# A two-block transformer kernel: the first gate and up pair reads x times scale, TensorE sums the shift's modulation weights, VectorE adds the squares

## The chip, the cores and the metric

The kernel runs on one core of one Trainium2 chip, in one launch. The metric is the device time of that launch in microseconds (us): 1558.38 us is the median of three timed runs of the kernel before (1555.36 to 1558.40). The profiled execution, from which all rows below come, took 1553.17 us, of which 1551.5 us are the span between its first and last recorded instruction.

## The reference, cut to what matters

The whole function is a first block (modulated SwiGLU, a hybrid mixer, a second SwiGLU) and a second block, for 512 tokens of width 1024, all in float32. The change is in the first SwiGLU's entry and in the first two of the nine modulation vectors:

```python
cs = jax.nn.silu(c)                                   # 1024 numbers
mod = (cs @ w_ada[l] + b_ada[l]).reshape(B, N_MOD, D) # 9 vectors of 1024; w_ada is 1024 x 9216
sh1, sc1, gt1, ... = mod
h = modulate(rms_norm(x, g_ffn1[l]), sh1, sc1)        # rms_norm(x) * g * (1 + sc1) + sh1
x = x + HALF_STEP * gt1 * swiglu(h, w_gu1[l], w_down1[l])   # D_FF = 2816
# swiglu: g, u = split(h @ w_gu); (silu(g) * u) @ w_down
```

Since rms_norm multiplies each token by one number rs, a product h @ w can also be had as rs * ((x * g * (1 + sc1)) @ w) + sh1 @ w.

## The kernel before, in words

Activations stand transposed: xT is 8 tiles (kt 0 to 7) of 128 features by 512 tokens. A product in float32 accuracy is made from three TensorE matmuls in fp32r (`three`, L2035 to L2039): high part by high part, high weights by low activations, low weights by high activations. So every weight tile of 128 columns (8 x 128 x 128 numbers, 0.5 MB) is loaded into one of four slots of w_stage by SyncE (`load`, L474), its high part is copied by ScalarE (`hi`, L793) and its low part made by VectorE (`lo`, L1265), and TensorE then runs 24 matmuls of 512 columns on it (`project`). Two tiles, gate and up, give one tile of hidden units; the first SwiGLU has 22 of these in two halves.

Every order is written out by hand, engine by engine, with semaphores between them; there is no scheduler. At the start:

- POOL issues the loads of w_ada (L546), 8 tiles of 0.5 MB for each of the nine vectors into 8 slots of ada_w; vector number q = 0 is the scale (ADA_ORDER = [1, 0]), q = 1 the shift. SyncE issues c, ident, x (2 MB), some 20 rows of constants and then the w_gu tiles (L477).
- VectorE multiplies each w_ada tile by its eight numbers of silu(c) and adds it into ada_acc (`ada_add`, L1278 for the first and L1281 for the other seven tiles). TensorE sums over the 128 partitions with 8 matmuls with one column (`ada_reduce`, L2031), and VectorE adds the bias (`ada_col`, L1287) and makes gs = g * (1 + scale) (L1293).
- TensorE transposes x (L2004), ScalarE copies it (L910) and squares it (L803), TensorE sums the squares over all features (`norm_sum`, L2014), and ScalarE makes rs with Ln and Exp (L834, L836).
- `modulate`: VectorE makes x * gs * rs (L1305), ScalarE adds the shift and keeps the high part h_hi (L859), VectorE the low part h_lo (L1310), tile by tile.
- TensorE starts the first pair of gate and up (`project_pair`) with h_hi[0] and h_lo[0], then does the other pairs. VectorE multiplies the pair's results (L1344) after ScalarE's Silu (L877), and adds up the next modulation vectors between the pairs.

The mixer and the second SwiGLU already have another entry (`lead`, L2043): their first tile reads x times scale without rs, and its product is multiplied by rs and gets the shift's sum (L2058, 8 matmuls of one column) afterwards. There `norm_total` adds squares that VectorE has already added.

## Time and profile before

| | us |
|---|---|
| median of three timed runs | 1558.38 |
| profiled execution | 1553.17 |
| its span | 1551.5 |
| TensorE busy in the span | 1476.4 (95%) |
| VectorE busy | 886.0 (57%) |
| ScalarE busy | 616.9 (40%) |
| POOL busy | 381.5 (25%) |

TensorE (PE in the rows) is busy nearly everywhere but in the first of the profile's 40 slices. [...] A float32 matmul is recorded as two rows. What follows is therefore read from the first 66 us, engine by engine, and from what TensorE waits for afterwards.

### The profile page before, as it was taken

To read this page: it belongs to the slowest core of one execution; us is meant where nothing else is said; L and a number is where in the kernel's file an instruction comes from. 1 tells how busy PE (TensorE), PEld (TensorE's weight loads), DVE (VectorE), ACT (ScalarE), POOL (GpSimd) and SP (SyncE) were. 2 spreads that over 40 slices of the span, in tenths; PEclk is the share of its full clock that TensorE was granted. 3 is DMA by queue.
4 is the path that set the end of the run, shared out by engine and by line. 5 is a ranking of instruction groups with operands and counts; after the bars stand their busy time and mean duration, and the time that the engine had idled before them with its cause. 6 is when DMAs were issued, how large, how long until landed. Compare 5 with 4: busy or idle time off the path is not lost. (4 is left out here: it accounts for less than half of the span.)

```text
span 1551.5 us, 19059 instructions
## 1 busy us (share of the span) xinstructions
PE 1476.4 (95%) x7046; PEld 1164.2 (75%) x7046; DVE 886.0 (57%) x1264; ACT 616.9 (40%) x933; POOL 381.5 (25%) x492
## 2 busy tenths in 40 slices
PE   4999999999999999899999999999899999988997
PEld 3788888888777776468888888888677787766565
DVE  5767426533673576847434334432666547798974
ACT  3422213232544443745433113222531234777644
POOL 3111001000000000031006788400202100799910
PEclk9999999999999999999999999999999999999998
DMA  9887526323253222013333433453133223222211
GB/s 347 276 275 262 200 80 204 102 87 100 58 150 83 59 66 78 1 41 103 107 97 95 142 103 109 149 212 100 49 95 110 72 82 109 68 81 69 82 28 55
DMA packets 204710, 177.93 MB, mean 115 GB/s; under 512 B 7379, under 2 KB 184079, under 8 KB 204118
## 3 DMA queue, kind: packets, MB, share of 16 engines
q1 hardware_dynamic: 188438, 121.87, 26.5%
q0 software_dynamic: 15040, 52.89, 9.6%
q10 hardware_dynamic: 1152, 2.10, 0.4%
q8 instruction: 51, 0.84, 0.2%
q14 instruction: 29, 0.24, 0.0%
HBM read 168.37 MB, written 8.46 MB: 114 GB/s over the span
## 5 line engine op out<-in xcount | busy, mean ns | idle before, releaser
L2037 PE MATMUL ps<-h_hi,w_hi 128*128 128x512 f32 x1224 | 490.4, 401 | 17.0 <-DVE w_lo L1268 11.2
L2039 PE MATMUL ps<-h_hi,w_lo 128*128 128x512 f32 x1224 | 477.6, 390 | 0.0
L2038 PE MATMUL ps<-h_lo,w_hi 128*128 128x512 f32 x1224 | 477.5, 390 | 0.0
L1268 DVE TENSOR_TENSOR w_lo<-w_stage,w_hi 128x1024 fp32r<-128x1024 f32 x225 | 292.6, 1313 | 218.2 <-ACT w_hi L797 215.6
L797 ACT ACTIVATE w_hi<-w_stage 128x1024 fp32r<-128x1024 f32 x225 | 230.8, 1048 | 186.1 <-PE ps L2039 179.5
L2037 PEld LDWEIGHTS ps<-h_hi,w_hi 128*128 128x128 f32 x1224 | 230.1, 188 | 86.0 <-issue 36.9
L2038 PEld LDWEIGHTS ps<-h_lo,w_hi 128*128 128x128 f32 x1224 | 230.3, 188 | 49.0 <-issue 3.6
L2039 PEld LDWEIGHTS ps<-h_hi,w_lo 128*128 128x128 f32 x1224 | 230.1, 188 | 49.2
L2037 PE MATMUL ps<-a_hi,w_hi 128*128 128x512 f32 x544 | 213.1, 392 | 7.6 <-DVE a_lo L1965 3.9
L2039 PE MATMUL ps<-a_hi,w_lo 128*128 128x512 f32 x544 | 211.8, 389 | 0.0
L2038 PE MATMUL ps<-a_lo,w_hi 128*128 128x512 f32 x544 | 211.8, 389 | 0.0
L1344 DVE TENSOR_TENSOR tmp<-tmp,ps 128x512 f32<-128x512 f32 x44 | 30.3, 688 | 196.6 <-PE ps L2039 196.4
L2037 PEld LDWEIGHTS ps<-a_hi,w_hi 128*128 128x128 f32 x544 | 102.1, 188 | 31.3 <-issue 7.3
L879 ACT ACTIVATE a_hi<-tmp 128x512 fp32r<-128x512 f32 (+1 forms) x44 | 27.9, 633 | 234.1 <-DVE tmp L1344 234.1
L2039 PEld LDWEIGHTS ps<-a_hi,w_lo 128*128 128x128 f32 x544 | 102.1, 188 | 21.5
L2038 PEld LDWEIGHTS ps<-a_lo,w_hi 128*128 128x128 f32 x544 | 102.2, 188 | 20.8
L546 POOL DMA_DIRECT2D ada_w<-in_w_ada x72 | 38.6, 536 | 226.4 <-DVE ada_acc L1278 118.7
L781 POOL TENSOR_TENSOR pacc<-pacc,tmp 128x512 f32<-128x512 f32 x48 | 71.8, 1496 | 63.3 <-ACT tmp L1219 59.4
L1281 DVE SCALAR_TENSOR_TENSOR ada_acc<-ada_w,cs,ada_acc 128x1024 f32<-128x1024 f32 x63 | 80.8, 1283 | 9.7 <-DMA ada_w<-in_w_ada 7.9
L781 POOL TENSOR_TENSOR pacc<-pacc,sq 128x512 f32<-128x512 f32 x47 | 72.0, 1531 | 3.8
L1893 DVE SCALAR_TENSOR_TENSOR ps<-gb,cw,ps 128x512 f32<-128x512 f32 x105 | 71.0, 743 | 0.0
L877 ACT ACTIVATE tmp<-ps 128x512 f32<-128x512 f32 x43 | 25.7, 599 | 108.2 <-PE ps L2039 108.2
(436 smaller groups left out, 1500.2 us busy)
## 6 DMA issues: line engine op xcount, KB each, us to landing
w_stage<-in_w_gu SPq DMA_DIRECT2D x88, 512.0 KB, 4.2
ada_w<-in_w_ada POOLq DMA_DIRECT2D x72, 512.0 KB, 6.5
w_stage<-in_w_down SPq DMA_DIRECT2D x44, 512.0 KB, 3.7
w_stage<-in_w_in SPq DMA_DIRECT2D x24, 512.0 KB, 3.9
w_stage<-in_odd_w_in SPq DMA_DIRECT2D x24, 512.0 KB, 3.7
w_stage<-in_even_w_in SPq DMA_DIRECT2D x16, 512.0 KB, 3.8
w_stage<-in_w_out SPq DMA_DIRECT2D x8, 512.0 KB, 3.7
mats<-mats_d POOLq DMA_DIRECT2D x4, 1024.0 KB, 6.7
```

Source lines behind the costliest of these rows:

```text
L546: pool.dma_start(ada_w[:, kt], a["w_ada"][0][kt * P:(kt + 1) * P, bass.ds(j * D, D)]) \
L781: pool.tensor_tensor(pacc[:, t % 2], pacc[:, t % 2], tap_of[m % 4], ALU.add).then_inc(pool_tap, 1)
L797: act.activation(w_hi[:, c % RING], w_in[:, c % RING], ACT.Copy).then_inc(w_hi_ready, 1)
L877: act.activation(tmp[:, f % 2], ps[2 * (f % 2)][:], ACT.Silu).then_inc(silu_ready, 1)
L879: act.activation(a_hi[:, bass.ds(i * (2 * S) + f * S, S)], tmp2[:, f % 2], ACT.Copy) \
L1268: dve.tensor_tensor(w_lo[:, c % RING], w_in[:, c % RING], w_hi[:, c % RING].bitcast(F32), ALU.subtract).then_inc(w_split, 1)
L1281: dve.scalar_tensor_tensor(acc, ada_w[:, kt], cs[:, kt:kt + 1], acc, ALU.mult, ALU.add).then_inc(ada_done, 1)
L1344: dve.tensor_tensor(tmp2[:, f % 2], tmp[:, f % 2], ps[2 * (f % 2) + 1][:], ALU.mult) \
L1893: dve.scalar_tensor_tensor(acc, gb[:, t % 2, k:k + S], cw[:, t, k:k + 1], acc, ALU.mult, ALU.add).then_inc(tap_done, 1)
L2037: pe.matmul(bank, w_hi[:, slot, k], rhs_hi, start=start, stop=False, skip_group_check=True)
L2038: pe.matmul(bank, w_hi[:, slot, k], rhs_lo, start=False, stop=False, skip_group_check=True)
L2039: return pe.matmul(bank, w_lo[:, slot, k], rhs_hi, start=False, stop=stop, skip_group_check=True)
```

## The change: what it does

- The first pair (w_gu tiles 0 and 1) reads x times gs, as h_hi and h_lo, without rs and shift (`scaled_hi`, `scaled_lo`, new `lead_pair`). After it VectorE multiplies both results by rs, and the shift's sums over the two tiles' columns come in through rcol (Silu's bias, and an addend of the product with the up half).
- The shift's sums are 16 float32 matmuls of one column (new `shift_cols`), placed behind the first three steps of the second pair, since the shift must be known by then. The second pair (tiles 2 and 3, one after another before) now is a `project_pair` too, on the modulated h.
- The shift's own w_ada tiles are no longer added up by VectorE. TensorE does it (new `ada_rows`): for each of the 8 tiles and each half of 512 columns one float32 matmul with 32 weight columns, of which one is silu(c) and 31 are zero. The four tiles of a call go to four groups of 32 rows of a PSUM bank. ScalarE copies the two banks out, and `ada_reduce` sums over partitions as before. These matmuls stand inside the first pair, behind steps k = 3 and k = 4.
- The squares are added by VectorE, seven additions, and TensorE makes one matmul with ones where it made eight.
- POOL's loads of w_ada wait for c and ident; the shift's wait for the scale's last tile. SyncE's first w_gu load waits for the scale's tile 5, the fourth for the shift's tile 3, the fifth for the shift's sums.

The diff, cut to what the prediction speaks of:

```diff
--- before.py
+++ after.py
...
@@ -479,15 +483,17 @@
             def ffn(n):
                 for half in range(2):
                     t0, f0 = T_FFN[n] + half * 3 * HALF, half * HALF
+                    if t0 == 0:
+                        sp.wait_ge(ada_in[5], 16)
                     for j in range(2):
                         load(0, t0 + j, cols_of(w_gu[n], f0 * P + j * FF))
-                    if t0 == 0:
-                        sp.wait_ge(ada_done, 2 * KT - 2)
                     def pair_of_hidden(i):
                         for j in range(4):
-                            if n == 1 and isinstance(i, int) and j == 2:
-                                sp.wait_ge(shift_sum, 2)
+                            if t0 == 0 and isinstance(i, int) and j == 1:
+                                sp.wait_ge(ada_in[3], 32)
+                            if isinstance(i, int) and j == 2:
+                                sp.wait_ge(shift_sum, [1, 3][n])
                             load(i, t0 + 2 + j, cols_of(w_gu[n], i * (2 * P) + (f0 + 1 + j // 2) * P + j % 2 * FF))
                     rounds(sp, 0, HALF // 2, pair_of_hidden, peel=(half == 0))
...
@@ -546,9 +553,12 @@
                 pool.dma_start(ada_w[:, kt], a["w_ada"][0][kt * P:(kt + 1) * P, bass.ds(j * D, D)]) \
                     .then_inc(ada_in[kt], 16)
-            for q in range(2):
-                for kt in range(KT):
-                    ada_load(q, ADA_ORDER[q], kt)
+            pool.wait_ge(c_in, 32)
+            for kt in range(KT):
+                ada_load(0, ADA_ORDER[0], kt)
+            pool.wait_ge(ada_in[KT - 1], 16)
+            for kt in range(KT):
+                ada_load(1, ADA_ORDER[1], kt)
             for c in range(2):
                 pool.wait_ge(w_loaded[c], 16)
             with pool.Fori(2, 9) as j:
...
@@ -911,11 +918,20 @@
                 if kt:
                     act.wait_ge(x_ready, kt)
                     square(0, kt - 1)
-            for c in range(2):
-                hi(0, c)
+            hi(0, 0)
+            act.wait_ge(gs_ready, 1)
+            scaled_hi(0, gs)
+            hi(0, 1)
+            for kt in range(1, KT):
+                scaled_hi(kt, gs)
+            hi(0, 2)
+            act.preload_act_table_set("natural_log_exp_and_others")
+            act.wait_ge(ada_done, 2 * KT)
+            for half in range(2):
+                act.activation(ada_acc1[:, half * S:(half + 1) * S], ps[5 + half][:], ACT.Copy).then_inc(c_ready, 1)
             norm_rs(0)
+            hi(0, 3)
             act.wait_ge(mod_ready, 2)
-            act.wait_ge(gs_ready, 1)
             modulate(0, sublayer(0)[1])
             ffn(0, 1)
...
@@ -1298,12 +1314,20 @@
                 if m:
                     lo(0, [None, T_MIX, T_FFN[1]][m] + 2)
                 dve.wait_ge(rs_ready, n + 1)
+                if n == 0:
+                    lo(0, 2)
                 for kt in range(KT + 2):
                     if kt < KT:
                         if kt >= 4:
                             dve.wait_ge(h_ready, H_NORM[m] * KT + kt - 3)
                         dve.scalar_tensor_tensor(hn[kt % 4], xT[:, kt], scale[:, kt:kt + 1], rs[:],
                                                  ALU.mult, ALU.mult).then_inc(hn_ready, 1)
+                    if n == 0 and kt < 2:
+                        continue
+                    if n == 0 and kt == 2:
+                        ada_col(1, ADA_ORDER[1])
+                        lo(0, 3)
+                        dve.wait_ge(mod_ready, 2)
                     if kt >= 2:
                         j = kt - 2
                         dve.wait_ge(h_hi_ready, H_NORM[m] * KT + j + 1)
...
@@ -1334,15 +1358,21 @@
                     def hidden(i, f, q=None):
-                        for j in range(n == 1 and half == 0 and f == 0, 2):
+                        led = half == 0 and f == 0
+                        for j in range([2, 1][n] if led else 0, 2):
                             lo(i, t0 + 2 * f + 2 + j)
                             if q is not None:
                                 for k in range(2):
                                     ada_add(q, 4 * (f - 1) + 2 * j + k)
                         dve.wait_ge(silu_ready, i * 2 + (F0 + f + 1))
                         dve.wait_ge(w_used, i * 4 + (t0 + 2 * f + 2))
-                        dve.tensor_tensor(tmp2[:, f % 2], tmp[:, f % 2], ps[2 * (f % 2) + 1][:], ALU.mult) \
-                            .then_inc(prod_ready, 1)
+                        if led and n == 0:
+                            dve.wait_ge(lead_ready, 2)
+                            dve.scalar_tensor_tensor(tmp2[:, 0], sq[:, 0], rcol[:, 1:2], tmp[:, 0],
+                                                     ALU.add, ALU.mult).then_inc(prod_ready, 1)
+                        else:
+                            dve.tensor_tensor(tmp2[:, f % 2], tmp[:, f % 2], ps[2 * (f % 2) + 1][:], ALU.mult) \
+                                .then_inc(prod_ready, 1)
                         dve.wait_ge(a_hi_ready, i * 2 + (F0 + f + 1))
                         at = bass.ds(i * (2 * S) + f * S, S)
                         dve.tensor_tensor(a_lo[:, at], tmp2[:, f % 2], a_hi[:, at].bitcast(F32), ALU.subtract) \
...
@@ -1396,25 +1426,42 @@
                         scaled_lo(*[(H_LEAD[1], KT - 1, gs[:, KT:2 * KT]), (H_EVEN, KT - 1, gg)][n])
                     lo(0, t1 + 12)
-            dve.wait_ge(silu_c, 1)
-            for q in range(2):
-                for kt in range(KT):
-                    ada_add(q, kt)
-                    if q == 1 and kt == 0:
-                        dve.wait_ge(cols_t, 2)
-                        dve.tensor_copy(cols[:], ps[1][:, 0:N_COLS]).then_inc(cols_ready, 1)
-                        dve.wait_ge(cols_t, 3)
-                        dve.tensor_copy(bada[:], ps[2][:, 0:72]).then_inc(cols_ready, 1)
-                        dve.wait_ge(cols_ready, 2)
-                    if q == 1 and kt == KT // 2:
-                        ada_col(0, ADA_ORDER[0])
-            lo(0, 0)
-            lo(0, 1)
-            ada_col(1, ADA_ORDER[1])
-            dve.wait_ge(mod_ready, 2)
+            def add_squares(first, last):
+
+                for kt in range(first, last):
+                    dve.wait_ge(sq_ready, kt + 1)
+                    ins = dve.tensor_tensor(sq[:, 0], sq[:, 0] if kt > 1 else x_sq[:, 0], x_sq[:, kt], ALU.add)
+                    if kt < KT - 1:
+                        link(ins)
+                if last == KT:
+                    ins.then_inc(sq_added, 1)
+
+            dve.wait_ge(c_ready, 1)
+            for kt in range(KT):
+                ada_add(0, kt)
+            dve.wait_ge(cols_t, 2)
+            dve.tensor_copy(cols[:], ps[1][:, 0:N_COLS]).then_inc(cols_ready, 1)
+            dve.wait_ge(cols_t, 3)
+            dve.tensor_copy(bada[:], ps[2][:, 0:72]).then_inc(cols_ready, 1)
+            dve.wait_ge(cols_ready, 2)
+            add_squares(1, 4)
+            ada_col(0, ADA_ORDER[0])
+            dve.wait_ge(mod_ready, 1)
             scale_cols(0, G_FFN1)
             dve.wait_ge(gs_ready, 1)
+            lo(0, 0)
+            scaled_lo(H_LEAD[0], 0, gs)
+            lo(0, 1)
+            for kt in range(1, KT):
+                scaled_lo(H_LEAD[0], kt, gs)
+            add_squares(4, KT)
             modulate(0, 0, *sublayer(0))
+            dve.wait_ge(shift_sum, 1)
+            link(dve.tensor_copy(rcol[:, 0:2], ps[7][:, KT:KT + 2]))
+            dve.wait_ge(h_ready, (H_NORM[0] + 1) * KT)
+            dve.tensor_tensor(tmp[:, 0], ps[0][:], rs[:], ALU.mult).then_inc(lead_ready, 1)
+            dve.wait_ge(sq_used, SUMMED[0])
+            dve.tensor_tensor(sq[:, 0], ps[1][:], rs[:], ALU.mult).then_inc(lead_ready, 1)
             ffn(0, 0, True)
             def keep_v(v, bank):
...
@@ -2008,12 +2055,6 @@
             pe.transpose(ps[1][:, 0:N_COLS], rows[0:N_COLS, :], ident[0:N_COLS, 0:N_COLS]).then_inc(cols_t, 1)
             pe.transpose(ps[2][:, 0:72], rows2[0:72, :], ident[0:72, 0:72]).then_inc(cols_t, 1)
-            def norm_sum(n, kt):
-
-                pe.wait_ge(sq_ready, n * KT + kt + 1)
-                pe.matmul(ps[0][:], ones[:], sq[:, kt % 2], start=(kt == 0), stop=(kt == KT - 1)) \
-                    .then_inc(sq_used, 1)
-
             def norm_total(n, bank, acc):
                 if n == N_EVEN:
...
@@ -2059,6 +2102,48 @@
                                    start=(k == 0), stop=(k == KT - 1))
                 mm.then_inc(shift_sum, 1)
+            def ada_rows(first):
+
+                for kt in range(first, first + 4):
+                    pe.wait_ge(ada_in[kt], 32)
+                for half in range(2):
+                    for g in range(4):
+                        mm = pe.matmul(ps[5 + half][32 * g:32 * g + 32, :], cs_wide[:, first + g],
+                                       ada_w[:, first + g, half * S:(half + 1) * S], start=(first == 0), stop=(first == 4),
+                                       skip_group_check=True)
+                mm.then_inc(ada_done, 4)
+
+            def lead_pair():
+
+                for k in range(KT):
+                    pe.wait_ge(h_ready, H_LEAD[0] * KT + k + 1)
+                    for j in range(2):
+                        if k == 0:
+                            pe.wait_ge(w_split, j + 1)
+                        mm = three(ps[j][:], j, k, h_hi[:, k], h_lo[:, k], k == 0, k == KT - 1)
+                        if k == KT - 1:
+                            mm.then_inc(w_used, 1)
+                    if k < KT - 1:
+                        mm.then_inc(pair_read, 1)
+                    if k == 3:
+                        ada_rows(0)
+                    if k == 4:
+                        ada_rows(4)
+                    if k == 6:
+                        ada_reduce(1)
+                        pe.wait_ge(sq_added, 1)
+                        pe.matmul(ps[3][:], ones[:], sq[:, 0], start=True, stop=True).then_inc(sq_used, 1)
+                pe.wait_ge(mod_ready, 2)
+
+            def shift_cols(first, last):
+
+                for m in range(first, last):
+                    j, k = divmod(m, KT)
+                    mm = pe.matmul(ps[7][:, KT + j:KT + j + 1], w_in[:, j, k], sublayer(0)[1][:, k:k + 1],
+                                   start=(k == 0), stop=(k == KT - 1))
+                if last == 2 * KT:
+                    mm.then_inc(shift_sum, 1)
+
             def project_pair(c, h_from, bank0=0):
                 pe.wait_ge(w_split, c + 2)
...
@@ -2068,6 +2153,8 @@
                         mm = three(ps[bank0 + j][:], (c + j) % RING, k, h_hi[:, k], h_lo[:, k], k == 0, k == KT - 1)
                         if k == KT - 1:
                             mm.then_inc(w_used, 1)
+                    if c == 2 and k < 3:
+                        shift_cols(6 * k, min(6 * k + 6, 2 * KT))
             def ffn(n, norm_before, norm_after, ada, aside=None):
                 for half in range(2):
...
@@ -2076,6 +2163,9 @@
                     def hidden(i, f):
+                        if t0 == 0 and f == 1 and isinstance(i, int) and i == 0:
+                            project_pair(2, H_NORM[0] * KT, 2)
+                            return
                         if n == 1 and half == 0 and f == 1 and isinstance(i, int) and i == 0:
                             project_pair(t0 + 1, H_NORM[2] * KT, 1)
                             project(0, t0 + 3, 3)
...
```

What stands in TensorE's queue where the scale's and shift's sums were, before:

```order
L2009 MATMUL ps<-ident,rows_142 128x72
L2014 MATMUL ps<-sq,ones 128x512 [waits sq_ready,x_ready]
L2014 MATMUL ps<-sq,ones 128x512 [waits sq_ready] x7
L2031 MATMUL ps<-ones,ada_acc 128x1 [waits ada_done,cols_ready,x_ready]
L2031 MATMUL ps<-ones,ada_acc 128x1 x7
L2031 MATMUL ps<-ones,ada_acc_140 128x1 [waits mod_ready,ada_done]
L2031 MATMUL ps<-ones,ada_acc_140 128x1 x7
L2037 MATMUL ps<-h_hi,w_hi 128x512 [waits h_ready,w_split]
```

In the changed kernel, the same queue from the end of step k = 6 of the first pair to the start of the second pair:

```order
L2074 MATMUL ps<-ones,ada_acc_142 128x1 [waits mod_ready,c_ready,ada_done]
L2074 MATMUL ps<-ones,ada_acc_142 128x1 x7
L2135 MATMUL ps<-sq,ones 128x512 [waits sq_added]
L2080 MATMUL ps<-h_hi,w_hi 128x512 [waits h_ready]
L2081 MATMUL ps<-h_lo,w_hi 128x512
L2082 MATMUL ps<-h_hi,w_lo 128x512
L2080 MATMUL ps<-h_hi,w_hi 128x512
L2081 MATMUL ps<-h_lo,w_hi 128x512
L2082 MATMUL ps<-h_hi,w_lo 128x512
L2080 MATMUL ps<-h_hi,w_hi 128x512 [waits h_ready,w_split,mod_ready]
L2081 MATMUL ps<-h_lo,w_hi 128x512
```

The shift's reduction and the sum of squares have moved from ahead of the first pair to between its steps 6 and 7, and the second pair now waits for the shift (mod_ready) and for modulated tiles (h_ready).

VectorE's queue ahead of the first modulated tile h_lo, before:

```order
L1268 TENSOR_TENSOR w_lo<-w_stage,w_hi 128x1024 [waits w_hi_ready] x2
L1287 TENSOR_TENSOR mod<-ps,bada 128x8 [waits ada_sum]
L1293 SCALAR_TENSOR_TENSOR gs<-mod,cols 128x8 [waits mod_ready]
L1305 SCALAR_TENSOR_TENSOR tmp<-xT,gs,rs 128x512 [waits rs_ready,gs_ready]
L1305 SCALAR_TENSOR_TENSOR tmp<-xT,gs,rs 128x512
L1305 SCALAR_TENSOR_TENSOR tmp_69<-xT,gs,rs 128x512
L1310 SCALAR_TENSOR_TENSOR h_lo<-tmp,mod,h_hi 128x512 [waits h_hi_ready]
```

And in the changed kernel, from the last squares on:

```order
L1433 TENSOR_TENSOR sq<-sq,x_sq 128x512 [waits sq_ready,dve_self] x3
L1284 TENSOR_TENSOR w_lo<-w_stage,w_hi 128x1024 [waits w_hi_ready,rs_ready]
L1323 SCALAR_TENSOR_TENSOR tmp<-xT,gs,rs 128x512 x2
L1323 SCALAR_TENSOR_TENSOR tmp_69<-xT,gs,rs 128x512
L1303 TENSOR_TENSOR mod<-ps,bada 128x8 [waits ada_sum]
L1284 TENSOR_TENSOR w_lo<-w_stage,w_hi 128x1024 [waits w_hi_ready]
L1334 SCALAR_TENSOR_TENSOR h_lo<-tmp,mod,h_hi 128x512 [waits h_hi_ready,mod_ready]
```

The three products with rs, the shift's column and the two low parts of w_gu tiles 2 and 3 all stand behind the wait for rs_ready and ahead of the first h_lo.

SyncE's first weight loads (w_gu tiles 0 to 4) in the changed kernel:

```order
L476 DMA rows_144<-in_b_ada 72x128
L481 DMA w_stage<-in_w_gu 128x8x128 [waits ada_in5]
L481 DMA w_stage<-in_w_gu 128x8x128 x2
L481 DMA w_stage<-in_w_gu 128x8x128 [waits ada_in3]
L481 DMA w_stage<-in_w_gu 128x8x128 [waits w_split,shift_sum]
```

Before, tiles 0 and 1 waited for nothing, and tile 4 for its slot alone.

## Rows read from the trace of the kernel before

**Rows 1.** The page's 40 slices of the span: busy tenths of TensorE, DMA share.

```profile
PE   4999999999999999899999999999899999988997
...
DMA  9887526323253222013333433453133223222211
```

**Rows 2.** Windows of the start: busy us (x instructions) per engine, PEclk, DMA share, GB/s.

```profile
20.00:30.00 10.00, 9.31 (x32) 4.17 (x32) 8.27 (x9) 5.28 (x10) 1.74 (x3) 1.00 1.04 390
30.00:40.00 10.00, 4.05 (x21) 3.88 (x20) 7.80 (x11) 4.85 (x6) 4.13 (x8) 0.58 1.04 337
60.00:80.00 20.00, 20.00 (x98) 16.86 (x97) 15.29 (x17) 6.27 (x8) 3.82 (x8) 1.00 0.91 298
```

**Rows 3.** Timeline, TensorE: start us, us, line, operation, count [idle before <-releaser].

```profile
14.54 5.32 PE L2004 MATMUL ps<-ident,x_rows 128*128 128x128 f32 x32 [10.71 <-DMA x_rows<-in_x]
20.90 7.90 PE L2014 MATMUL ps<-sq,ones 128*128 128x512 f32 x16
28.63 1.84 PE L2031 MATMUL ps<-ones,ada_acc 128*128 128x1 f32 x16
34.98 3.58 PE L2031 MATMUL ps<-ones,ada_acc 128*128 128x1 f32 x16 [4.51 <-DVE ada_acc L1281]
41.88 0.76 PE L2037 MATMUL ps<-h_hi,w_hi 128*128 128x512 f32 x1 [3.32 <-DVE h_lo L1310]
46.25 0.39 PE L2037 MATMUL ps<-h_hi,w_hi 128*128 128x512 f32 x1
48.32 0.39 PE L2037 MATMUL ps<-h_hi,w_hi 128*128 128x512 f32 x1
```

**Rows 4.** Timeline, VectorE, same columns.

```profile
21.29 1.28 DVE L1281 SCALAR_TENSOR_TENSOR ada_acc<-ada_w,cs,ada_acc 128x1024 f32<-128x1024 f32 x1 [0.25 <-DMA ada_w<-in_w_ada]
33.64 1.28 DVE L1281 SCALAR_TENSOR_TENSOR ada_acc<-ada_w,cs,ada_acc 128x1024 f32<-128x1024 f32 x1 [0.32 <-DMA ada_w<-in_w_ada]
38.59 0.17 DVE L1287 TENSOR_TENSOR mod<-ps,bada 128x8 f32<-128x8 f32 x1 [1.40 <-PE ps L2031]
38.99 2.08 DVE L1305 SCALAR_TENSOR_TENSOR tmp<-xT,gs,rs 128x512 f32<-128x512 f32 x3
40.99 0.75 DVE L1310 SCALAR_TENSOR_TENSOR h_lo<-tmp,mod,h_hi 128x512 fp32r<-128x512 f32 x1
49.60 2.35 DVE L1268 TENSOR_TENSOR w_lo<-w_stage,w_hi 128x1024 fp32r<-128x1024 f32 x2
65.59 0.69 DVE L1344 TENSOR_TENSOR tmp<-tmp,ps 128x512 f32<-128x512 f32 x1 [1.54 <-PE ps L2039]
```

**Rows 5.** Single microseconds around the clock's changes: TensorE busy, PEclk, DMA share, GB/s.

```profile
31.00:32.00 1.00, 0.00 (x0) 0.77 1.01 377
32.00:33.00 1.00, 0.00 (x0) 0.50 1.08 329
...
44.00:45.00 1.00, 1.00 (x3) 0.50 1.05 393
45.00:46.00 1.00, 1.00 (x5) 0.91 1.12 408
```

**Rows 6.** Timeline, ScalarE.

```profile
31.76 1.06 ACT L797 ACTIVATE w_hi<-w_stage 128x1024 fp32r<-128x1024 f32 x1 [4.15 <-DMA w_stage<-in_w_gu]
36.47 0.69 ACT L834 ACTIVATE rs<-ps,eps 128x512 f32<-128x512 f32 x1
37.19 0.63 ACT L836 ACTIVATE rs<-rs 128x512 f32<-128x512 f32 x1
```

**Rows 7.** Groups by line and shape, TensorE, whole span: count | busy us, mean ns.

```profile
L2511 PE MATMUL ps<-gb,dgc 128*128 128x512 f32 x48 | 20.9, 592 | 0.0
...
L2058 PE MATMUL ps<-mod,w_stage 128*128 128x1 f32 x16 | 1.8, 245 | 0.0
```

**Rows 8.** Groups by shape between 644.4 and 646.4 us, TensorE: 64 weight columns, alternating halves.

```profile
L2305 PE MATMUL ps<-pt_a,va 128*64 128x256 f32 x16 | 1.9, 385 | 0.0
```

**Rows 9.** DMA issues up to 50 us: count, KB each, median us to landing.

```profile
w_stage<-in_w_gu SPq DMA_DIRECT2D x6, 512.0 KB, 15.0
x_rows<-in_x SPq DMA_DIRECT2D x1, 2048.0 KB, 12.5
```

**Rows 10.** What TensorE waits for after 66 us: us in total, times, longest.

```profile
PE ps L2037 <- DVE w_lo L1268: 11.4, 12, 1.6
PE ps L2291 <- ACT pt_a L1047: 7.4, 6, 2.2
```

More of the change, by code:

```diff
@@ L61, in added @@
     last = KT - 2
-    return (n - 1 - (n > N_EVEN)) * last + kt
-SUMMED = {1: KT + 1, 2: KT + 2, N_FIN: KT + 3, N_ODD: KT + 4, N_LAST: KT + 5}
+    return 1 + (n - 1 - (n > N_EVEN)) * last + kt
+SUMMED = {0: 1, 1: 2, 2: 3, N_FIN: 4, N_ODD: 5, N_LAST: 6}
 SH, GP, LEVELS = 16, 16, 9
@@ L160, in constants @@
             "swap": swap, "head_ones": heads, "pick": pick}
-H_LEAD, H_NORM, H_EVEN, H_ODD = [None, 1, 3], [0, 2, 4], 5, 6
+H_LEAD, H_NORM, H_EVEN, H_ODD = [0, 2, 4], [1, 3, 5], 6, 7
 def read_by_lead(m, k):
-    return ([None, 0, 1][m] * (KT - 1)) + k + 1
+    return m * (KT - 1) + k + 1
 def upto(eng, sem, value):
@@ L364, in build_program @@
         x_rows = put("x_rows", [P, ST, D])
+        put = region(at_of["a_lo"] + KT * S * 4, S * 4)
+        cs_wide = put("cs_wide", [P, KT, 32])
+        put = region(at_of["a_lo"], KT * S * 4)
+        x_sq = put("x_sq", [P, KT, S])
         ada_w = sb("ada_w", [P, KT, D])
@@ L541, in _ @@
             pool.memset(eps[:], EPS).then_inc(zeroed, 1)
+            pool.memset(cs_wide[:], 0.0).then_inc(zeroed, 1)
             def ada_load(q, j, kt):
@@ L790, in _ @@
             act.wait_ge(cols_t, 1)
-            act.activation(cs[:], ps[7][:, 0:KT], ACT.Silu).then_inc(silu_c, 1)
+            act.activation(cs[:], ps[7][:, 0:KT], ACT.Silu).then_inc(c_ready, 1)
+            act.wait_ge(zeroed, 4)
+            act.activation(cs_wide[:, :, 0], ps[7][:, 0:KT], ACT.Silu).then_inc(c_ready, 1)
             def hi(i, c):
@@ L827, in norm_rs @@
             def norm_rs(n):
-                if n == 0:
-                    act.preload_act_table_set("natural_log_exp_and_others")
-                    act.wait_ge(sq_used, KT)
-                else:
-                    act.wait_ge(sq_used, SUMMED[n])
-                act.activation(rs[:], ps[{0: 0, N_ODD: 3}.get(n, 1)][:], ACT.Ln, bias=eps[:], scale=1.0 / D).then_inc(ln_ready, 1)
+                act.wait_ge(sq_used, SUMMED[n])
+                act.activation(rs[:], ps[{0: 3, N_ODD: 3}.get(n, 1)][:], ACT.Ln, bias=eps[:], scale=1.0 / D).then_inc(ln_ready, 1)
                 act.wait_ge(ln_ready, n + 1)
@@ L854, in modulate @@
                     act.wait_ge(hn_ready, m * KT + kt + 1)
-                    if m and kt < KT - 1:
+                    if kt < KT - 1:
                         act.wait_ge(pair_read, read_by_lead(m, kt))
-                    elif m:
-                        act.wait_ge(w_used, [None, T_MIX, T_FFN[1]][m] + 1)
+                    else:
+                        act.wait_ge(w_used, [1, T_MIX, T_FFN[1]][m] + 1)
                     act.activation(h_hi[:, kt], hn[kt % 4], ACT.Identity, bias=shift[:, kt:kt + 1]) \
@@ L866, in hidden @@
                     def hidden(i, f):
-                        led = n == 1 and half == 0 and f == 0
-                        for j in range(led, 2):
+                        led = half == 0 and f == 0
+                        for j in range([2, 1][n] if led else 0, 2):
                             hi(i, t0 + 2 * f + 2 + j)
                         if led:
-                            act.wait_ge(lead_ready, 2)
+                            act.wait_ge(lead_ready, [1, 4][n])
                             act.activation(tmp[:, 0], tmp[:, 0], ACT.Silu, bias=rcol[:, 0:1]).then_inc(silu_ready, 1)
@@ L1334, in hidden @@
                     def hidden(i, f, q=None):
-                        for j in range(n == 1 and half == 0 and f == 0, 2):
+                        led = half == 0 and f == 0
+                        for j in range([2, 1][n] if led else 0, 2):
                             lo(i, t0 + 2 * f + 2 + j)
@@ L1970, in _ @@
             modulate(2, 2, *sublayer(2))
-            dve.wait_ge(shift_sum, 2)
+            dve.wait_ge(shift_sum, 3)
             link(dve.tensor_copy(rcol[:, 0:1], ps[7][:, 0:1]))
@@ L2001, in _ @@
                 if kt == KT - 1:
-                    pe.wait_ge(silu_c, 1)
+                    pe.wait_ge(c_ready, 2)
                 for st in range(ST):
@@ L2028, in ada_reduce @@
                 pe.wait_ge(ada_done, q * KT + KT)
+                if isinstance(q, int) and q == 1:
+                    pe.wait_ge(c_ready, 4)
                 upto(pe, mod_ready, q)
@@ L2098, in ffn @@
                     else:
-                        project_pair(t0, 0)
+                        lead_pair()
                     with_ada = [HALF // 2, 2][half] if ada else 0
@@ L2129, in ffn @@
                             mm.then_inc(down_done, 1)
-            for kt in range(KT):
-                if kt == 0:
-                    pe.wait_ge(x_ready, 1)
-                norm_sum(0, kt)
             pe.wait_ge(x_ready, KT)
@@ L2137, in _ @@
             ada_reduce(0)
-            ada_reduce(1)
             ffn(0, 0, 1, True)
@@ L2199, in sums @@
                         pe.wait_ge(gcol_ready, 1)
[L2200 removed]
+                        pe.wait_ge(zeroed, 5)
                     if i % 4 == 0:
```

18 lines of the change are left out of this document (9 added, 9 removed).

## The prediction

> **What bounds the kernel now.** I began with the page's 40 slices [rows 1]: TensorE stands at 9 or 8 tenths in every slice but the first, where it is 4, and there the DMA engines are full. So time can be won only where TensorE idles, and matmul time added anywhere lengthens the run. The windows [rows 2] show that the idle time is mostly before 42 us: in 30 to 40 us it is busy 4.05 of 10 us, at a mean granted clock of 0.58, while the DMA engines are at 390 and 337 GB/s.
>
> The timelines give the chain [rows 3, 4]. VectorE adds the scale's last w_ada tile at 21.29, the shift's at 33.64. TensorE reduces the scale at 28.63 in 1.84 us and the shift at 34.98 in 3.58 us; VectorE has mod at 38.59, begins x * gs * rs at 38.99, the first h_lo at 40.99, and TensorE starts the first pair at 41.88. From there on it does not stop: the four w_gu tiles of the first two pairs, 96 matmuls, are through when VectorE takes the last one at 65.59. That is 23.7 us, one start at half clock included. Everything later hangs on this stream, so I compare that one time, 65.6 us, with its counterpart in the changed kernel.
>
> **The start.** The first pair now needs the scale alone. x and the scale's eight tiles are 2.1 + 4.2 = 6.3 MB, at 390 GB/s [rows 2] 16.1 us; x is issued at about 2 us and is flowing by 3.7, so they are in at about 19.8. POOL's loads start some 2 us later than before, behind c and ident, but the w_gu tiles no longer share the engines. VectorE's last addition of the scale ended at 21.29 + 1.28 = 22.6 before [rows 4]; I put it at 22.0. Copying cols and bada with their wait takes 0.7, since TensorE waits for them: reduction from 22.7. It took 1.84 us at full clock and 3.58 at half [rows 3]. The clock fell from 1.00 to 0.77 at 31 to 32 us and to 0.50 in the next microsecond, when TensorE had done nothing since 30.5 [rows 3, 5]; here it is idle for some 4 us before the reduction, so I take 3.6: 26.3. The column and gs take 0.4 (38.59 to 38.99 [rows 4]), the low part of tile 0 half of 2.35, or 1.2, the first low part of h 0.75, TensorE's start 0.15. The three squares added ahead of the column lie beside the reduction. Start of the first pair: 26.3 + 2.5 = 28.8, against 41.9: **13.1 us earlier**. Ends: 27 with the reduction at full clock, 31 if the weights are late.
>
> **What TensorE gets in return**, in order:
>
> - ada_rows, 16 float32 matmuls of 512 columns with 32 weight columns. No row shows 32 columns. With 128 weight columns one row of the two costs 20.9/48 = 0.435 us [rows 7], so 32 rows one after another are 13.9 us: upper end. If four groups of columns ran abreast, 13.9/4 = 3.5: lower end. Nearest is L2305 [rows 8]: 64 weight columns, alternating halves of the array, 256 columns, 16 rows in 1.9 us, 0.119 each where 0.435/2 = 0.218 would be serial: a factor 0.55, nearly two abreast, although each row alone is recorded with 385 ns. [...] This saves VectorE 8 additions, which is worth nothing once TensorE is the bound.
> - ada_reduce(1), formerly in TensorE's idle time, now in the stream: 1.8 (clock up). The one matmul with ones: 0.9. The eight norm sums that go, 7.90 us [rows 3], were idle time already: worth nothing.
> - A new wait. Behind the matmul with ones come Ln 0.69 and Exp 0.63 [rows 6], 1.6 with semaphores; then on VectorE, queued behind rs_ready, the low part of tile 2, 1.2; three products with rs, 2.1; the shift's column 0.2; the low part of tile 3, 1.2; h_lo 0.75; TensorE 0.15: 7.2 us [rows 4]. TensorE has only step k = 7 beside it: matmuls 9 apart stand at 46.25 and 48.32 [rows 3], 0.23 each, six are 1.4. It stands for **5.8 us**, and all of its queue with it. Ends 4.8 and 6.8.
> - A second start at half clock. The first ran at 0.50 from 41.88 to past 45 us [rows 5], 3.2 us, costing 1.6. Here six one-column matmuls (1.4 at full clock) stand between steps k = 0 and 1, which run slow as well. 1.6 to 4; I take 2.5.
> - shift_cols: 16 float32 matmuls, 32 rows, at 1.8/16 [rows 7] = 3.6.
> - Tile 4 of w_gu may only be loaded when the shift's sums are done, about 69 us; landing, ScalarE's high and VectorE's low part end near when TensorE asks: 0 to 1.5, I take 0.7.
>
> Sum: 28.8 + 23.7 + 7.6 + 1.8 + 0.9 + 5.8 + 2.5 + 3.6 + 0.7 = 75.4 us, against 65.6: **9.8 us later**. The rescaling by rs, rcol and the Silu table come on VectorE and ScalarE while the second pair runs, 11 us, and are covered; without cover they would cost 3. Afterwards the streams are equal. Profiled execution: 1553.2 + 9.8 = 1563. The three timed runs of before have their median 5.2 us above the profiled one, so I forecast on their scale 1558.4 + 9.8 = 1568.
>
> The rows bear out two abreast. [...]
>
> **The rivals.**
>
> 1. The column groups run four abreast: ada_rows 3.5 instead of 7.6, so 4.1 less: 5.7 later, 1564. For it: L2305 overlaps at all. [...]
> 2. They do not overlap, and each matmul with its new tile pays in full: 13.9, so 6.3 more: 16 later, 1574.5. Against it is L2305 again.
> 3. The weights set the start. The first six w_gu loads took 15.0 us in the median to land [rows 9], and tile 0 was there only at 31.76 [rows 6], issued at 9: beside w_ada loads a w_gu load crawls. Now tiles 0 to 2 are asked for near 17 us, and the shift's loads start near 20. If tile 1 comes at 30 instead of 25, the pair's second half starts 3 us late: 1571. [...]
> 4. The other side: not slower. The 9.8 us are given back downstream, in a wait of TensorE for something that does not hang on TensorE. Place: after 66 us; price: all 9.8 must fit, 1558. TensorE's greatest waits there are 11.4 us in 12 pieces for w_lo and 7.4 in 6 for pt_a [rows 10], which follow TensorE's own releases of slots and banks; only if most of them were for transfers at a pace of their own, more than 6.7 us of them, would it come within 0.2%. To be faster through an earlier start, that start would have to be at 19 us or before, when the scale's tiles have not landed.
> 5. The change does not do what it says: the first pair still waits for the shift, through the wait for tile 4 or the slots. Then nothing is won at the start; 13 us more, 1581. Against: the queue's waits name only h_ready and w_split.
>
> **How the numbers follow.** Forecast 0.54, rival 1 0.20, rival 2 0.09, rival 3 0.07, rival 4 0.06, rival 5 0.02, a faster outcome from something unseen 0.02. Cheap ends together (start 27, rows 3.5, wait 4.8, cold 1.6, no wait for tile 4) come to 66.9 us, 1.3 later, 1560; but they must all meet. The range is 1560 to 1577: below it lie rival 4 and noise, above it rival 5 and dear ends together. A change under 0.2% (3.1 us) cannot be told from none: slower 0.88, same 0.08, faster 0.04.
>
> **What would show it.** Start of the first pair's matmuls near 29 us (right: 27 to 31). The 16 matmuls of ada_rows: two blocks of 3.8 us each, or 1.8, or 7. TensorE idle for nearly 6 us between the pairs, released by h_lo, with PEclk 0.50 after it. VectorE's addition of w_ada tiles 8 fewer. The counterpart of 65.59 at 75. I am wrong if the idle time between the pairs is under 3 us, or if the ada_rows cost less than 3, or if the rest of the run shortens by what the start lost.

## The result, and the profile after

The changed kernel takes 1571.91 us (median of 4 runs, 1569.47 to 1573.87) where the kernel before takes 1557.34 beside it: a ratio of 1.0097, 95% interval 1.0081 to 1.0114, or 14.6 us slower. Forecast were 1568 in a range of 1560 to 1577, and 9.8 us slower. The profiled execution took 1569.47 us, its span 1567.8, 16.3 us longer than the span before. The direction and the range held; the sum was right in parts, and one wait of TensorE was not in it at all.

TensorE's timeline of the changed kernel answers to [rows 3]: start, duration, line, operation, count, idle time before and its releaser. In the rows DVE is VectorE, ACT ScalarE, SP SyncE; PEclk is the clock granted to TensorE as a share of full speed, and half clock is 0.50. The same reduction of 16 rows took 1.84 us at 1.00 and 3.58 us at 0.50 [rows 3].

```profile
22.65 3.54 PE L2074 MATMUL ps<-ones,ada_acc 128*128 128x1 f32 x16 [4.50 <-DVE bada L1445]
28.65 0.79 PE L2080 MATMUL ps<-h_hi,w_hi 128*128 128x512 f32 x1 [2.45 <-DVE h_lo L1351]
...
36.88 1.92 PE L2111 MATMUL ps<-ada_w,cs_wide 128*32 128x512 f32 x16
...
40.34 1.92 PE L2111 MATMUL ps<-ada_w,cs_wide 128*32 128x512 f32 x16
...
48.85 0.39 PE L2082 MATMUL ps<-h_hi,w_lo 128*128 128x512 f32 x1
54.52 0.77 PE L2080 MATMUL ps<-h_hi,w_hi 128*128 128x512 f32 x1 [5.28 <-DVE h_lo L1334]
...
57.21 1.79 PE L2142 MATMUL ps<-mod,w_stage 128*128 128x1 f32 x12
...
81.46 0.39 PE L2082 MATMUL ps<-h_hi,w_lo 128*128 128x512 f32 x1
...
86.03 3.57 PE L2074 MATMUL ps<-ones,ada_acc 128*128 128x1 f32 x16 [4.18 <-DVE ada_acc L1297]
89.47 0.77 PE L2080 MATMUL ps<-h_hi,w_hi 128*128 128x512 f32 x1
```

The first pair starts at 28.65 where it started at 41.88. Sixteen rows of ada_rows, eight float32 matmuls, are done in 1.92 us. TensorE then stands for 5.28 us between the pairs, and once more, for 4.18 us, ahead of the reduction of modulation vector 2, released by VectorE's last addition. Before, that reduction followed on its tile without a gap, at full clock:

```profile
75.97 0.40 PE L2039 MATMUL ps<-h_hi,w_lo 128*128 128x512 f32 x1
76.20 1.84 PE L2031 MATMUL ps<-ones,ada_acc 128*128 128x1 f32 x16
77.91 0.48 PE L2037 MATMUL ps<-h_hi,w_hi 128*128 128x512 f32 x1
```

So the same points can be laid side by side:

| us | before | after | difference |
|---|---|---|---|
| end of TensorE's matmuls on tile 5 | 76.4 | 81.9 | 5.5 |
| start of the reduction of vector 2 | 76.2 | 86.0 | 9.8 |
| first matmul of tile 6 | 77.9 | 89.5 | 11.6 |
| VectorE takes the product of tiles 6 and 7 | 89.09 | 103.52 | 14.4 |

```profile
89.09 0.69 DVE L1344 TENSOR_TENSOR tmp<-tmp,ps 128x512 f32<-128x512 f32 x1 [3.41 <-PE ps L2039]
```

```profile
103.52 0.69 DVE L1374 TENSOR_TENSOR tmp<-tmp,ps 128x512 f32<-128x512 f32 x1 [6.82 <-PE ps L2082]
```

The last 2.8 us of the 14.4 are matmuls at half clock. The windows of the changed kernel (stretch, its length, TensorE busy (x instructions), PEclk, DMA share, GB/s) show it:

```profile
84.00:85.00 1.00, 0.00 (x0) 1.00 0.95 360
85.00:86.00 1.00, 0.00 (x0) 0.67 0.86 315
86.00:88.00 2.00, 1.97 (x10) 0.50 0.94 282
...
92.00:94.00 2.00, 2.00 (x6) 0.50 0.75 220
94.00:96.00 2.00, 2.00 (x7) 0.61 1.01 335
```

From there the distance stays at 14.4 (170.77 before, 185.20 after). It grows to 16.0 in this pair of profiles through one more fall of the clock, from 187 us on, after the last reduction of that half and 0.9 us of idle time that both kernels have; the matching stretch of before stayed at 1.00. e7 below had such a fall too with before's entry, so the fall does not need the change.

Why VectorE is late is in its own timeline of the changed kernel, with TensorE's first matmul on tile 4 put in by time:

```profile
34.28 2.87 DVE L1433 TENSOR_TENSOR sq<-sq,x_sq 128x512 f32<-128x512 f32 x4
49.28 1.23 DVE L1284 TENSOR_TENSOR w_lo<-w_stage,w_hi 128x1024 fp32r<-128x1024 f32 x1 [12.13 <-ACT rs L843]
50.43 2.07 DVE L1323 SCALAR_TENSOR_TENSOR tmp<-xT,gs,rs 128x512 f32<-128x512 f32 x3
...
64.04 0.16 DVE L1460 COPY rcol<-ps 128x2 f32<-128x2 f32 x1 [1.72 <-PE ps L2142]
...
67.17 0.69 DVE L1378 TENSOR_TENSOR a_lo<-tmp,a_hi 128x512 fp32r<-128x512 f32 x1 [0.70 <-ACT a_hi L886]
69.20 1.23 DVE L1284 TENSOR_TENSOR w_lo<-w_stage,w_hi 128x1024 fp32r<-128x1024 f32 x1 [1.34 <-ACT w_hi L809]
70.81 0.39 PE L2080 MATMUL ps<-h_hi,w_hi 128*128 128x512 f32 x1
76.11 0.68 DVE L1374 TENSOR_TENSOR tmp<-tmp,ps 128x512 f32<-128x512 f32 x1
...
83.31 2.67 DVE L1297 SCALAR_TENSOR_TENSOR ada_acc<-ada_w,cs,ada_acc 128x1024 f32<-128x1024 f32 x2
85.89 0.68 DVE L1374 TENSOR_TENSOR tmp<-tmp,ps 128x512 f32<-128x512 f32 x1
```

The same points before:

```profile
57.05 1.23 DVE L1268 TENSOR_TENSOR w_lo<-w_stage,w_hi 128x1024 fp32r<-128x1024 f32 x1 [0.26 <-ACT w_hi L797]
65.32 0.39 PE L2037 MATMUL ps<-h_hi,w_hi 128*128 128x512 f32 x1
72.79 2.67 DVE L1281 SCALAR_TENSOR_TENSOR ada_acc<-ada_w,cs,ada_acc 128x1024 f32<-128x1024 f32 x2
```

In the changed kernel VectorE stands idle for 12.13 us waiting for rs, while TensorE does VectorE's former additions. Then it takes up tile 4 at 69.20, 1.6 us ahead of TensorE's 70.8; before it took it up at 57.05, 8.3 us ahead of TensorE's 65.3. What follows for VectorE is the same in both, four low parts and eight additions between them, 16.8 us to the last addition in the changed kernel, against 10.9 us of matmuls on tiles 4 and 5. Before, the lead covered the difference.

Two waits stand right ahead of 69.20, and both hang on the shift's sums, which TensorE has done at 64.0: VectorE's for rcol (1.72 us), and the one for tile 4's high part (1.34 us), since SyncE loads tile 4 only when the shift's sums are done and ScalarE waits for that load:

```profile
68.10 1.06 ACT L809 ACTIVATE w_hi<-w_stage 128x1024 fp32r<-128x1024 f32 x1 [0.97 <-DMA w_stage<-in_w_gu]
```

No run here loads tile 4 earlier, so what this alone would give back is not shown.

### The profile page after: what moved, and what is told of

It is laid out like the page before. It is cut to its first block and busy times, and to the rows that moved or that the text cites. A ratio compares the mean times of both kernels' runs of the same rounds, so it can differ in the third digit from the quotient of the medians.

```text
span 1567.8 us, 19191 instructions
## 1 busy us (share of the span) xinstructions
PE 1487.2 (95%) x7096; PEld 1174.1 (75%) x7096; DVE 889.1 (57%) x1274; ACT 623.9 (40%) x944; POOL 381.7 (24%) x493
## 5 line engine op out<-in xcount | busy, mean ns | idle before, releaser
L1297 DVE SCALAR_TENSOR_TENSOR ada_acc<-ada_w,cs,ada_acc 128x1024 f32<-128x1024 f32 x56 | 71.9, 1283 | 2.4 <-DMA ada_w<-in_w_ada 0.5
```

The costliest lines, as they stand in the source:

```text
L1297: dve.scalar_tensor_tensor(acc, ada_w[:, kt], cs[:, kt:kt + 1], acc, ALU.mult, ALU.add).then_inc(ada_done, 1)
```

## The experiments

Times are medians beside the kernel before on the same chip; the ratios are to that kernel. The changed kernel stands at 1.0097.

**e1: the reduction of vector 2 one tile later.**

```diff
+    if t0 == 0 and isinstance(i, int) and i == 1:
+        pe.wait_ge(prod_ready, 2)
+        project(1, 2, 2)
+        ada_reduce(2)
+        project(1, 3, 3)
...
+    if q is not None and not (t0 == 0 and isinstance(i, int) and i == 0):
```

The two projects are tiles 6 and 7; the other vectors are reduced where they were.

> Changed kernel with one edit: TensorE's reduction of modulation vector 2 stands behind w_gu tile 6 instead of behind tile 5, where TensorE waited 4.2 us for VectorE's last addition and then went on at half clock. Theory (VectorE is one pair late, and this single wait costs some 9 us with the half clock after it): 1571.9 - 7 to 9 = 1563 to 1565, clock 1.00 through 80 to 100 us, at most 1.5 us of waiting at the reduction of vector 3. Rival (the lag of VectorE only moves the wait on, to the weights' low parts or to the next reduction): a wait of 4 us turns up later and the time stays within 3 us of 1572.

Measured: 1568.55 us, ratio 1.0080 (1.0067 to 1.0093). The wait of 4.2 us is gone; the reduction of vector 3 waits 0.5. Yet only some 2 us are won by the medians, where 7 to 9 were expected, and this interval overlaps the changed kernel's. Neither theory had the reason. These are the windows of e1 where the changed kernel had 0.66, 1.00 and 1.00:

```profile
50.00:60.00 10.00, 6.12 (x21) 0.63 0.15 61
60.00:70.00 10.00, 10.00 (x35) 0.50 0.02 4
70.00:80.00 10.00, 10.00 (x39) 0.84 1.13 305
```

Half clock stands from 53 to 73 us, and TensorE is busy throughout from 53.9 on. What stands in its queue there is the same as in the changed kernel, where the clock was back at 58. After a wait of the same 5.28 us half clock lasted until 58 us in the one profile and until 73 us in the other. e9 tests whether this ate the gain.

**e2: rs ahead of the shift.**

```diff
                     if k == 3:
                         ada_rows(0)
+                        pe.wait_ge(sq_added, 1)
+                        pe.matmul(ps[3][:], ones[:], sq[:, 0], start=True, stop=True).then_inc(sq_used, 1)
                     if k == 4:
                         ada_rows(4)
-                    if k == 6:
+                    if k == 5:
                         ada_reduce(1)
-                        pe.wait_ge(sq_added, 1)
-                        pe.matmul(ps[3][:], ones[:], sq[:, 0], start=True, stop=True).then_inc(sq_used, 1)
...
-                        ada_col(1, ADA_ORDER[1])
                         lo(0, 3)
+                        ada_col(1, ADA_ORDER[1])
```

On ScalarE norm_rs(0) and hi(0, 3) stand ahead of the copies of the shift's sums.

> Changed kernel with the matmul with ones moved from behind step k = 6 to behind the first four w_ada tiles, ScalarE's Ln and Exp and tile 3's high part ahead of its copies of the shift's sums, VectorE's low part of tile 3 ahead of the shift's column, and the shift's reduction behind k = 5 instead of k = 6. Theory (the 5.3 us between the two pairs are the chain rs, low part, three products, column, low part, h_lo): the gap closes to under 1 us, the second pair runs at full clock, 5.3 + 1.6 = 7 us less, 1565; the later wait of 4.2 us for VectorE stays. Rival (the gap is set by the shift's column, not by rs): the gap shrinks by no more than 2 us and the time is 1570 or more.

Measured: 1563.12 us, ratio 1.0044 (1.0031 to 1.0057), 7 to 8 us less than the changed kernel (7.2 by the medians over before, 8.2 by the ratios). TensorE's waits in e2 from 30 to 230 us, in total, times, longest:

```profile
PE ps L2074 <- DVE ada_acc L1297: 4.3, 1, 4.3
PE ps L2080 <- issue: 0.9, 1, 0.9
PE ps L2080 <- DVE w_lo L1284: 0.2, 1, 0.2
```

The wait of 5.3 us for h_lo is gone. The edit brings rs and the shift's reduction forward together and so does not part them; the changed kernel's timeline does: VectorE waits for rs until 49.28 and works without a gap from there to the first h_lo, the shift's column among it, 5.5 us after its sums were done (46.9). So it was the chain behind rs. The wait for VectorE's addition is still there: they are two waits.

**e3: the w_ada matmuls one after another.**

```diff
-    mm = pe.matmul(ps[5 + half][32 * g:32 * g + 32, :], ..., start=(first == 0), stop=(first == 4),
+    mm = pe.matmul(ps[5 + half][0:32, :], ..., start=(first + g == 0), stop=(first + g == 7),
```

ScalarE copies 32 rows of each bank instead of 128, into an ada_acc set to zero, so that the sums stay the same.

> Changed kernel with all 16 w_ada matmuls of TensorE in one group of 32 columns and 32 PSUM rows, the other rows set to zero, so that the same sums are made. Theory (in the changed kernel four column groups run abreast, 1.9 us for eight matmuls): each block of eight takes 7.0 us, 10 us more in all, 1582; VectorE then has no more lag than before relative to TensorE, so the wait at the reduction of vector 2 stays near 4 us. Rival (the 32-column matmuls are short in themselves, since few columns are loaded): the blocks stay at 1.9 to 2.5 us and the time within 2 us of 1572.

Measured: 1580.11 us, ratio 1.0165 (1.0151 to 1.0180), 24.4 us over the kernel before. Its timeline:

```profile
36.49 7.05 PE L2112 MATMUL ps<-ada_w,cs_wide 128*32 128x512 f32 x16
```

7.05 us against 1.92: four column groups run abreast, a factor of 3.7, and narrow matmuls are not short by themselves (7.05/8 = 0.88 us; with 128 weight columns it is two rows of 0.435 [rows 7], 0.87). The wait at the reduction was 1.9 us, not the expected 4; TensorE ran at half clock from 64 to 84 us here, which gives VectorE time.

**e4: the first step without modulation vectors.**

```diff
-    rounds(dve, 0, with_ada, lambda i: two(i, i + [2, 7][half]), peel=(t0 == 0))
+    if t0 == 0:
+        two(0, None)
+        rounds(dve, 1, with_ada, lambda i: two(i, i + 1))
+    else:
+        rounds(dve, 0, with_ada, lambda i: two(i, i + 6))
```

Here two(i, q) is one step of two pairs in which vector q is added up and reduced; None is no vector. The same stands on TensorE, with_ada is 3 in the second half, and the first half's end waits for 6 vectors.

> Changed kernel in which VectorE and TensorE make no modulation vector beside pairs 1 and 2 (tiles 2 to 5); vectors 2 to 5 are made beside the next four steps and 6 to 8 beside the first three of the second half. Theory (ten us of VectorE's additions in the first step, begun one pair late, make TensorE wait): no wait at tile 5, 9 us less, 1563, perhaps 1 less still since the sums that follow stay clear. Rival (the clock falls there whatever VectorE does, after the one-column matmuls): the wait goes but half clock shows between 80 and 100 us, and only 4 us are won, 1568.

Measured: 1563.46 us, ratio 1.0062 (1.0044 to 1.0080); no wait for an addition, one of 0.6 us for a low part, clock 1.00 from 60 to 176 us. The medians say 7 us of gain over the changed kernel (14.6 against 7.7 over before), the ratios 5.4; both intervals together allow some 2 to 9, an estimate from their widths. It agrees with the theory, a little under the 9 expected. Its six executions ran from 1561.2 us, at a granted clock of 0.991 over the whole span, to 1570.4, at 0.982: the granted clock of one and the same kernel differed from execution to execution.

**e5: e2 and e4 together.**

> Changed kernel with the edits of e2_rs_before_shift and e4_first_pairs_without_sums together. Theory (the two waits are separate and each was some 7 us): 14.6 - 7.4 - 7.0 = 0 to 1 us over the kernel before, 1556; TensorE has no wait over 1 us between 30 and 230 us. That leaves the earlier start (13.2) spent on the added TensorE work (w_ada matmuls 4.1, shift's reduction 1.7, ones 0.9, column sums 3.9) and a rest. Rival (the waits overlap, so that only one of them pays): 1562.

Measured: 1554.86 us (12 runs), ratio 0.9997 (0.9989 to 1.0006). TensorE's waits from 30 to 230 us are down to one:

```profile
PE ps L2084 <- issue: 0.9, 1, 0.9
```

So without the two waits and the half clock behind them the change neither wins nor loses: they are the whole of the loss, and the earlier start pays for the work that TensorE took over.

**e6: the waits filled with work that nobody reads.**

```diff
+    def filler(count):
+        for _ in range(count):
+            pe.matmul(ps[4][:], ones[:], xT[:, 0], start=True, stop=True)
...
+    filler(5)
     pe.wait_ge(mod_ready, 2)
...
+    if t0 == 0 and isinstance(i, int) and i == 0:
+        filler(4)
     if q is not None:
         ada_reduce(q)
```

The first stands ahead of the wait between the pairs, the second ahead of the reduction of vector 2.

> Changed kernel with idle TensorE kept busy by matmuls whose results nobody reads: five float32 matmuls of 512 columns (4.4 us) between the two pairs, where it waits 5.3 us, and four (3.5 us) ahead of the reduction of vector 2, where it waits 4.2 us. All waits stay, only the half clock after them can go. Theory (the stretches at 0.50 after the two waits cost 1.6 and 1.7 + 3.2 us): 1571.9 - 6 = 1565 to 1567, clock 1.00 from 60 to 100 us. Rival (the cost is the waits themselves): within 2 us of 1572.

Measured: 1564.27 us, ratio 1.0064 (1.0050 to 1.0078), some 6 us less by the medians over before, 2 to 9 by the widths of the intervals. The clock is at 1.00 from 34 to 230 us, the stretch around 187 us too. The waits' own dependences were left as they were: from the matmul with ones to the second pair it is 7.75 us here and 7.77 in the changed kernel. So about 6 of the 14.6 us are clock.

**e7: the same edit as e4 in the kernel before.**

> Kernel before with the edit of e4_first_pairs_without_sums alone: no modulation vector is made beside pairs 1 and 2. Theory (before, VectorE ended its additions ahead of TensorE's reduction, so there is nothing to win): within 2 us of the kernel before, 1554 to 1558. Rival (the sums in the first step cost something in any order, so e4's gain says nothing of the change): 4 us or more faster.

Measured: 1558.47 us (12 runs), ratio 1.0018 (1.0009 to 1.0028): 3 us slower, not faster. The additions beside the first pairs cost nothing with the old entry, so e4's gain belongs to the change. The 3 us are more than the theory's 2. The profile has a fall of the clock to 0.50 at 172 to 174 us, which may be these 3 us or not; a single profile does not settle it, nor whether e4 and e5 carry such a cost too.

**e8: e5 with TensorE kept busy at the start.** filler(5) stands ahead of the scale's reduction, ada_reduce(0), and filler(2) behind it.

> e5_both_waits_gone with five float32 matmuls of 512 columns, read by nobody, after the transposes of the constants and two after the scale's reduction, so that TensorE comes to the reduction and to the first pair at full clock. Theory (reduction 1.8 instead of 3.5, first pair without the slow start of 1.6): 3 us less than e5, 1552 to 1553, and faster than the kernel before by 2 to 4 us. Rival (the clock falls in the gap of 2.4 us ahead of the first pair all the same, or in a later one): within 1 us of e5.

Measured: 1552.85 us (12 runs), ratio 0.9988 (0.9979 to 0.9998). Its timeline shows the scale's reduction in 1.92 us and the first pair at a granted clock of 1.00 (26 to 30 us):

```profile
22.78 1.92 PE L2078 MATMUL ps<-ones,ada_acc 128*128 128x1 f32 x16 [0.75 <-DVE bada L1449]
...
27.24 0.50 PE L2084 MATMUL ps<-h_hi,w_hi 128*128 128x512 f32 x1 [0.71 <-DVE h_lo L1351]
27.57 0.40 PE L2085 MATMUL ps<-h_lo,w_hi 128*128 128x512 f32 x1
```

It is the one version here that is clear of the kernel before: 2.7 us faster by the medians, at least 0.3 by the interval. Against e5, 12 runs each, it is 2.0 us.

**e9: e1 with the filler between the pairs.**

> e1_sum_behind_tile6 with five float32 matmuls of 512 columns, read by nobody, in TensorE's 5.3 us between the two pairs. In e1's trace the wait for VectorE was gone, but half clock stood from 53 to 73 us, 20 us where the changed kernel had 7. Theory (e1 won the wait and lost it again to the longer half clock): without it the median is 1.6 + 8 us under e1's 1568.6, at 1559 to 1561, and clock 1.00 from 50 to 100 us. Rival (the sum's new place costs TensorE time in itself): 1565 or more.

Measured: 1560.02 us, ratio 1.0034 (1.0021 to 1.0047). Its windows against those of e1:

```profile
50.00:60.00 10.00, 9.01 (x47) 1.00 0.16 64
60.00:70.00 10.00, 10.00 (x50) 1.00 0.81 212
```

Five idle-time matmuls are worth 8 us here: e1 had won the wait and lost it to 20 us at half clock. In 60 to 70 us e1 has 35 matmuls where e9 has 50, and the reduction of vector 2, behind tile 6 in both, starts at 93.86 us in e1 and at 84.63 in e9. The later fall of e1's clock, to 0.53 in 114 to 116 us behind the reduction of vector 3, is not in e9's profile either.

**e10: the filler between the pairs alone.**

> Changed kernel with the same five matmuls between the two pairs only. Theory: the first wait's half clock is worth 2 to 5 us (its length differs from run to run), the second's stays: 1567 to 1570, in the profile the wait of 4.2 us for VectorE and half clock after it as before. Rival (filling the first wait also clears the second stretch): 1565 or less, as e6.

Measured: 1567.20 us, ratio 1.0079 (1.0066 to 1.0092), the wait of 4.2 us and half clock from 85 to 92 us as in the changed kernel. By the medians over before that is about 3 us for the first stretch, and some 3 for the second (e6 less e10). Neither is clear of the noise: the intervals of e10 overlap both the changed kernel's and e6's.

## Why the prediction was right, and where it was not

- **The start: right.** The first pair starts at 28.65 against 28.8 us, by the steps given: the last scale addition ended at 22.2 (22.0), the reduction ran at half clock in 3.54 (3.6), gs and the low parts took 2.5.
- **The first start at half clock: dearer, and not in the sum.** The 23.7 us held one such start of 3.2 us. Here half clock lasts from 28.65 to 34 us, and the fourteenth matmul starts 5.6 us after the first instead of 4.6: 1.0 more.

```profile
33.93 0.49 PE L2080 MATMUL ps<-h_hi,w_hi 128*128 128x512 f32 x1
```

- **ada_rows: mis-sized.** The two blocks cost 3.9 us with the start of the next matmul, where 7.6 stood in the sum. The 7.6 is 13.9 us times the factor 0.55 of the two groups in [rows 8], carried over to four groups; no run shows that term. What the runs showed in its place: a block took 1.92 us with four groups and 7.05 us in one group (e3), two blocks thus 3.84 us against 14.1, a factor of 0.27. Carrying two groups' factor over to four is the step that failed. Rival 1 had the size (3.5).
- **The shift's reduction, the matmul with ones, the column sums: right.** 1.7, 0.9 and 3.6 (at full clock) against 1.8, 0.9 and 3.6.
- **The wait between the pairs: right in place and size**, 5.3 against 5.8; VectorE's timeline and e2 show that the chain named was the one.
- **The second start at half clock: 1.7 against 2.5** in the profile. The profiled execution is the fastest of the four, so the others may have paid more: e10 wins about 3 us by its medians, not clear of the noise, by removing it, and in e1 it lasted 20 us.
- **Tile 4: 0 against 0.7.** TensorE did not wait; VectorE did, 1.34 us, and this was the beginning of the next point.
- The way to the end of the four tiles was thus 5.5 us longer and not 9.8; the forecast was some 4 too dear. (The terms as measured, -13.2 + 1.0 + 3.9 + 1.7 + 0.9 + 5.3 + 1.7 + 3.6, give 4.9; the rest lies in slower first matmuls behind a block, 0.50 us at 38.73 and 42.19 and 0.80 at 47.29, where the others take 0.39.) The sign that the prediction named came out all the same, by luck: VectorE takes the product of tiles 2 and 3, at 65.59 before, at 76.11 here, where 75 was forecast. TensorE was through with these tiles at 70.8; VectorE came to them 5.3 us late, busy with additions.
- **"Afterwards the streams are equal": wrong.** This is the step that failed in the mechanism. The rescaling and rcol were said to be covered by the second pair. TensorE did not wait for them, but behind them VectorE still had the additions of vector 2, with a lead over TensorE cut from 8.3 us to 1.6. TensorE waited 4.2, reduced at half clock (3.57 us against 1.84, 1.7 more) and ran 2.8 us longer on tile 6: 8.9 in all. No rival had it. A wait was looked for only at h_ready and w_split, and not at ada_done, although the kernel has TensorE take vector 2 right behind tile 5, and one addition costs VectorE 1.28 us [rows 4]. e4, e5 and e7 show the cost and to whom it belongs.
- The profile pair's other 1.9 us are mostly the clock's fall at 187 us.

So the 4 us too many and the missing 8.9 offset each other by half, and the forecast was nearer than its reasons: with rival 1's size for ada_rows, which was the true one, the sum would have said 1564. That the time fell close to 1568 is luck in that part. Of the 14.6 us, e2 says some 7 to 8 for the first wait with its clock, e4 some 5 to 7 for the second; e6 says that about 6 of both are clock. The rivals of late weights and of the change not doing what it says are refuted by the start at 28.65 us, with no idle time of TensorE inside the first pair; that of giving back downstream, by TensorE's waits after 90 us, which are in total those of before within 0.5 us for each of the larger releasers (11.4 and 11.4 us for w_lo, 7.4 and 7.6 for pt_a, 3.9 and 4.3 for a_lo). Rival 2, one after another, is refuted by the 1.92 us.

What stays open is why half clock lasted until 58 us in one profile and until 73 in another after the same wait with the same work. Each profile is one execution, and e4's six executions lie 9 us apart with their clocks, so it need not be the kernel that decides; but e1's five runs, all at 0.982 to 0.987, and e9's nine, at 0.989 to 0.993, say that for e1 the long stretch was no single accident.

## What to carry to other kernels

When a chain is moved off the start, ask of each engine how far ahead of the bounding engine it is afterwards, and follow its queue to the next thing that the bound waits for: a lead can be spent without any wait at the place of the change. Work moved into the bound's stream was paid in full here (3.9, 1.7, 0.9 and 3.6 us), and an engine with 12 us of idle time beside it is a reason to ask whether the wrong one has the work or the wrong order; that VectorE should have kept the shift's additions is argued here, no run tried it. Order short chains so that a result that could be had early (rs: the squares are added up at 37 us) is not queued behind one that arrives late (the shift): in e2 that was 7 to 8 us.

## What the runs showed of the hardware

- Four groups of 32 weight columns ran abreast in float32: eight matmuls of 512 columns in 1.92 us, against 7.05 in one group (e3), a factor of 3.7. Two groups of 64 columns gave a factor of 1.8 [rows 8].
- Half clock after the same wait of 5.3 us lasted until 58 us in the changed kernel and until 73 in e1, with TensorE busy in both. Matmuls whose results nobody reads, put in the wait, kept 1.00 and were worth 8 us there (e9 against e1) and 2 at the start (e8 against e5); the 3 in e10 are not clear of the noise.
- In the changed kernel TensorE idled from 81.9 (81.46 + 0.39), after 27 us of matmuls without a wait; the granted clock was still 1.00 at 84 to 85 us and was 0.67 in the next microsecond. At the start of before it fell at 31 to 32, when TensorE had idled only since 30.5 but had run one-column matmuls ahead of it [rows 3, 5]. In e1 it fell behind one-column matmuls with an idle time of only 0.45 us ahead of them (112.60), and in e9, behind the same, it did not.
